# One stationary block for both parts of the sample tokens, and one ones-product per norm, in a two-layer hybrid decoder step

## What is computed

```python
def rmsnorm(x, g):
    y = x32 * lax.rsqrt(jnp.mean(x32 * x32, axis=-1, keepdims=True) + NORM_EPS)
    return (y * g).astype(x.dtype)

def token_mixer(h, ...):
    hq, hf, hi, hg, nq, kc, vc, ks, vs, kw, vw, ngate, mgate = jnp.split(h @ w_in, splits, axis=-1)
    o_hg = hgrn2_mixer(hq, hf, hi, hg, ...)      # gated linear attention, 4 heads; hi are its values
    o_nsa = ...                                  # attention over compressed, selected and window keys
    return merged @ w_out
x = x + token_mixer(rmsnorm(x, norm_mix[l]), ...)
x = x + conv_ffn(rmsnorm(x, norm_ffn[l]), ...)
```

## Time and profile before

| | us |
|---|---|
| median of 3 runs | 1172.31 |
| the runs | 1170.33 to 1174.61 |
| profiled execution, first to last instruction (span) | 1170.5 |
| TensorE busy | 1152.3 |
| VectorE busy | 706.3 |
| ScalarE busy | 544.3 |
| GpSimd busy | 173.2 |
| DMA, mean share of the 16 engines | 45% |

### The profile page before, as it was taken

One profiled execution on the slowest core, in us unless ns is written; L12 is line 12 of the kernel. 1 busy time (PEld: TensorE's weight loads), 2 busy tenths in 40 slices (PEclk: granted clock), 3 DMA queues, 4 the chain that ended last, 5 costly groups with the idle time before them and its releaser, 6 DMA issues.

```text
span 1170.5 us, 21146 instructions
## 1 busy us (share of the span) xinstructions
PE 1152.3 (98%) x8625; PEld 1039.7 (89%) x8625; DVE 706.3 (60%) x1303; ACT 544.3 (47%) x867; POOL 173.2 (15%) x300
## 2 busy tenths in 40 slices
PE   8999999999999999999999999999999999999997
PEld 6987776778999999999999787677899999999997
DVE  5686355557566777763568643544756677776442
ACT  4542265553355555533444234755534555554231
POOL 1154300011120001000114450000312111010000
PEclk7999999989999999999999999999999999999998
DMA  9554332347644444334456525213784445432401
GB/s 282 159 163 173 107 113 73 109 118 206 226 144 144 144 146 150 123 123 159 144 127 206 175 78 173 73 37 100 217 268 155 138 151 163 152 109 90 174 32 45
DMA packets 151498, 165.99 MB, mean 142 GB/s; under 512 B 31492, under 2 KB 114214, under 8 KB 151078
## 3 DMA queue, kind: packets, MB, share of 16 engines
q1 hardware_dynamic: 151402, 164.64, 45.0%
HBM read 156.22 MB, written 12.46 MB: 144 GB/s over the span
## 4 chain that ended last, share of the span: by engine, by line
PE 94%; DVE 2%; DMA 2%; ACT 1%; SPq 1%; issue 0%; DVEq 0%; ACTq 0%
PE mm L671 66%; PE ax L671 23%; PE ax L674 4%; DMA ring<-in_state_hgrn 1%; DMA ring<-in_state_conv 1%; ACT mixb L1328 1%; DVE ring_low L1684 0%; DVE mixb L1835 0%; DVE mixb L2100 0%; SPq L481 0%; DVE work_parts L2069 0%; PE mm L674 0%; DVE mixb L1852 0%; DVE mixb L2101 0%; DVE mixb L2254 0%
## 5 line engine op out<-in xcount | busy, mean ns | idle before, releaser
L671 PE MATMUL mm<-work_parts 128*128 128x320 f32 (+2 forms) x1120 | 357.4, 319 | 1.1 <-DVE h_low L1678 1.1
L1684 DVE TENSOR_TENSOR ring_low<-ring,work_parts 128x2048 fp32r<-128x2048 f32 (+2 forms) x116 | 256.0, 2207 | 125.3 <-ACT work_parts L1328 124.6
L671 PE MATMUL mm<-h_low,work_parts 128*128 128x320 f32 x1024 | 320.1, 313 | 0.0
L671 PE MATMUL mm<-work_parts,ring_low 128*128 128x320 f32 x1024 | 316.2, 309 | 0.0
L1328 ACT ACTIVATE work_parts<-ring 128x2048 fp32r<-128x2048 f32 (+2 forms) x116 | 211.9, 1827 | 159.7 <-PE mm L671 90.3
L671 PEld LDWEIGHTS mm<-work_parts 128*128 128x128 f32 (+1 forms) x1120 | 209.8, 187 | 9.4 <-issue 2.2
L671 PEld LDWEIGHTS mm<-h_low,work_parts 128*128 128x128 f32 x1024 | 193.7, 189 | 0.3
L671 PEld LDWEIGHTS mm<-work_parts,ring_low 128*128 128x128 f32 x1024 | 193.8, 189 | 0.0
L671 PE MATMUL ax<-act_parts,work_parts 128*128 128x320 f32 x544 | 127.3, 312 | 0.6 <-DVE ring L2091 0.6
L671 PE MATMUL mm<-act_parts,work_parts 128*128 128x320 f32 x480 | 117.4, 310 | 0.0
L671 PE MATMUL mm<-hT,ring 128*128 128x320 f32 x384 | 110.4, 439 | 0.0
(11 more groups left out here) (238 smaller groups left out, 1597.1 us busy)
## 6 DMA issues: line engine op xcount, KB each, us to landing
ring<-in_w_gate_up SPq DMA_DIRECT2D x44, 1024.0 KB, 6.6
ring<-in_w_in SPq DMA_DIRECT2D x10, 2048.0 KB, 8.5
ring<-in_w_in SPq DMA_DIRECT2D x18, 1024.0 KB, 5.5
ring<-in_w_down SPq DMA_DIRECT2D x8, 1536.0 KB, 6.7
ring<-in_w_out SPq DMA_DIRECT2D x4, 2048.0 KB, 13.9
ring<-in_w_down SPq DMA_DIRECT2D x4, 2048.0 KB, 8.0
ring<-in_w_in SPq DMA_DIRECT2D x32, 128.0 KB, 3.1
ring<-in_cache_cmp_kv SPq DMA_DIRECT2D x32, 128.0 KB
```

Source lines behind the costliest of these rows:

```text
L671: return nc.tensor.matmul(out, lhsT, rhs, start=start, stop=stop)
L1684: V.tensor_tensor(unit_of(u, ring_r), unit_of(u, ring), unit_high(u).bitcast(F32), ALU.subtract).then_inc(*st.up(w_low[l]))
```

## The change

`token_rows` takes the sample block another way. GpSimd copies the sample columns of `h_high` and `h_low` side by side into `row_parts` (64 and 64 columns per feature tile). They are one stationary block of 128 columns, and one product with the high weights and one with the low weights take the place of three. The bank's upper 64 partitions then hold what the low activations gave; ScalarE writes them, scaled, and VectorE adds the scaled lower 64 (`sample_rows`). So VectorE now empties `hi2` and `kvn2`. (The fourth product, low by low, is added to the sum by this.) `row_scales` makes the sample factors twice, one under the other. The rest concerns the norms: GpSimd adds all eight squares, one product with ones is left, and that of norm 1 moves from ahead of `hf1` into the middle of it.

```diff
-NADD = 6
-    ... [(f"{x}{i}", "A") for x in ("hi", "kvn", "kvc") for i in range(3)]
+    out += [(f"{x}{i}", "V" if i == 2 and x != "kvc" else "A") for x in ("hi", "kvn", "kvc") for i in range(3)]
...
 def norm1_sums():                                   # square_sums (norm 2) likewise
                 pe.wait_ge(squares_added, 2 * L + 1)
-                mm(bank[:, 0:T], ones, sq[:, NADD - 1, :], True, False)
-                for k in range(NADD, KD):
-                    pe.wait_ge(squares[L], k + 1)
-                    last = mm(bank[:, 0:T], ones, sq[:, k, :], False, k == KD - 1)
-                last.then_inc(ax_full[L], 1)
+                mm(bank[:, 0:T], ones, sq[:, KD - 1, :], True, True).then_inc(ax_full[L], 1)
...
 def token_rows(name, u0, half):
+                pe.wait_ge(row_parts_ready, L + 1)
                 pe.wait_ge(w_low[L], u + 1)
...
-                        last = split_products(bank[0:TM[i], :], h_high[:, k, rows], h_low[:, k, rows], high[:, kk, :],
-                                              low[:, kk, :], k == 0, k == KD - 1)
+                        if i < 2:
+                            last = split_products(bank[:, :], h_high[:, k, rows], h_low[:, k, rows], high[:, kk, :],
+                                                  low[:, kk, :], k == 0, k == KD - 1)
+                        else:
+                            mm(bank[:, :], sample_parts(k), high[:, kk, :], k == 0, False)
+                            last = mm(bank[:, :], sample_parts(k), low[:, kk, :], False, k == KD - 1)
...
 def row_scales():
-                for i in range(3):
-                    last = mm(bank[0:TM[i], i:i + 1], rs[:, P * i:P * i + TM[i]], ident[:, 0:1], True, True)
+                for i in range(2):
+                    mm(bank[:, i:i + 1], rs[:, P * i:P * i + P], ident[:, 0:1], True, True)
+                for y in range(2):
+                    last = mm(bank[SMP * y:SMP * y + SMP, 2:3], rs[:, SEQ:T], ident[:, 0:1], True, True)
...
 # TensorE, order of a layer
                 entry_tile("hf0", 0, 0, (entry_lo[L], 0))
-                norm1_sums()
                 for h in range(1, HH):
-                    entry_tile(f"hf{h}", h // 2, h % 2)
+                    entry_tile(f"hf{h}", h // 2, h % 2, None, norm1_sums if h == 1 else None)
...
 # ScalarE
+                def sample_rows_high(out, bank):
+                    A(out, bank[SMP:P, :], ACT.Copy, scale=rsc[SMP:P, 6:7]).then_inc(*st.up(high_rows[L]))
...
 # VectorE
+                def sample_rows(name, n, out):
+                    bank = take(MM[L], f"{name}2")
+                    ve.wait_ge(high_rows[L], n)
+                    V.scalar_tensor_tensor(out, bank[0:SMP, :], rsc[0:SMP, 6:7], out, ALU.mult, ALU.add).then_inc(
+                        *st.up(mm_dve[L]))
...
                     if 3 <= kk < 6:
                         split(HIU + kk - 2, l)
+                    if kk == 5:
+                        sample_rows("hi", 1, vH[0:SMP, 2, :])
                     if kk == 6:
...
+                        sample_rows("kvn", 2, stok[0:SMP, 2, :])
...
 # GpSimd
-                    for m in range(1, NADD):
+                    for m in range(1, KD):
...
                 link(G.memset(rH[:, :, :], 1.0))
+                po.wait_ge(entry_lo[L], KD)
+                for n, tiles in enumerate((slice(0, 6), slice(6, KD))):
+                    for x, src in enumerate((h_high, h_low)):
+                        last = G.tensor_copy(row_parts[n][:, :, x, :], src[:, tiles, SEQ:T])
+                last.then_inc(*st.up(row_parts_ready))
```

More of the change, by code:

```diff
@@ L116, in mm_plan @@
     out = [("par", "V")] + [(f"hf{h}", "V") for h in range(HH)] + [(f"hq{h}", "V") for h in range(HH)]
-    out += [(f"nq{m}", "V") for m in range(4)] + [(f"{x}{i}", "A") for x in ("hi", "kvn", "kvc") for i in range(3)]
+    out += [(f"nq{m}", "V") for m in range(4)]
+    out += [(f"{x}{i}", "V" if i == 2 and x != "kvc" else "A") for x in ("hi", "kvn", "kvc") for i in range(3)]
     out += [(f"hg{h}", "V") for h in range(HH)]
@@ L334, in hybrid_step, with sample_parts @@
         act_high, act_low = (part(act_r, NJ * T * n, NJ * T).rearrange("p (j t) -> p j t", j=NJ) for n in range(2))
+        row_parts = [nc.alloc_sbuf_tensor_at(f"row_parts{n}", [P, P * kn], F32R, offset=at)[:, :].rearrange(
+            "p (k x t) -> p k x t", k=kn, x=2) for n, (kn, at) in enumerate(((6, work_at + 4 * 8256), (2, mixb_at + 4 * 14080)))]
+        def sample_parts(k):
+            return row_parts[k // 6][:, k % 6].rearrange("p x t -> p (x t)")
         xin = part(mixb, 4096, 3 * D).rearrange("p (i c) -> p i c", i=3)
@@ L419, in hybrid_step @@
         s_ready, sn_ready, sqo_ready = lsem("state_ready"), lsem("new_state"), lsem("o_squares")
+        high_rows = lsem("sample_rows_of_high_parts")
         decayed, merged_ready, pre_ready = lsem("state_decayed"), lsem("merged_ready"), lsem("prefix_ready")
@@ L429, in hybrid_step @@
         oh_ready, sums_ready, rso_ready = sem("oh_parts_ready"), sem("o_square_sums"), sem("o_rs")
+        row_parts_ready = sem("sample_row_parts_ready")
         oh_raw, glast_ready = sem("oh_raw"), sem("glast_ready")
@@ L760, in split_products, with split_tile @@
                 return mm(out, low, x_high, False, stop)
-            def split_tile(R, name, u, h, x_high, x_low, tile_ready=None):
+            def split_tile(R, name, u, h, x_high, x_low, tile_ready=None, between=None):
                 bank = begin(R, name)
@@ L768, in split_tile @@
                         pe.wait_ge(tile_ready[0], tile_ready[1] + k + 1)
+                    if between is not None and k == kn // 2:
+                        between()
                     last = split_products(bank[:, 0:T], unit_high(u)[:, k, h, :], unit_of(u, ring_r)[:, k, h, :],
@@ L815, in row_scales, with entry_tile @@
                 pe.wait_ge(rs_ready[L], 1)
-                for i in range(3):
-                    last = mm(bank[0:TM[i], i:i + 1], rs[:, P * i:P * i + TM[i]], ident[:, 0:1], True, True)
+                for i in range(2):
+                    mm(bank[:, i:i + 1], rs[:, P * i:P * i + P], ident[:, 0:1], True, True)
+                for y in range(2):
+                    last = mm(bank[SMP * y:SMP * y + SMP, 2:3], rs[:, SEQ:T], ident[:, 0:1], True, True)
                 last.then_inc(ax_full[L], 1)
-            def entry_tile(name, u, h, tile_ready=None):
+            def entry_tile(name, u, h, tile_ready=None, between=None):
                 pe.wait_ge(w_low[L], u + 1)
-                split_tile(MM[L], name, u, h, h_high, h_low, tile_ready)
+                split_tile(MM[L], name, u, h, h_high, h_low, tile_ready, between)
             def queries(m):
@@ L1410, in layer @@
                     bank = take(MM[L], f"hi{i}")
-                    A(vH[0:TM[i], i, :], bank[0:TM[i], :], ACT.Copy, scale=rsc[0:TM[i], 4 + i:5 + i]).then_inc(
-                        *st.up(mm_act[L]))
+                    if i < 2:
+                        A(vH[:, i, :], bank[:, :], ACT.Copy, scale=rsc[:, 4 + i:5 + i]).then_inc(*st.up(mm_act[L]))
+                    else:
+                        sample_rows_high(vH[0:SMP, 2, :], bank)
                 split(KVU + 1, l)
@@ L1416, in layer @@
                     bank = take(MM[L], f"kvn{i}")
-                    A(stok[0:TM[i], i, :], bank[0:TM[i], :], ACT.Copy, scale=rsc[0:TM[i], 4 + i:5 + i]).then_inc(
-                        *st.up(mm_act[L]))
+                    if i < 2:
+                        A(stok[:, i, :], bank[:, :], ACT.Copy, scale=rsc[:, 4 + i:5 + i]).then_inc(*st.up(mm_act[L]))
+                    else:
+                        sample_rows_high(stok[0:SMP, 2, :], bank)
                 cached_rows(range(4, NSEQ))
@@ L1914, in layer @@
                         bank = take(AXR[L], "rst")
-                        V.tensor_copy(rsc[:, 4:6], bank[:, 0:2])
-                        V.tensor_copy(rsc[0:SMP, 6:7], bank[0:SMP, 2:3]).then_inc(*st.up(ax_dve[L]))
+                        V.tensor_copy(rsc[:, 4:7], bank[:, 0:3]).then_inc(*st.up(ax_dve[L]))
                     if h == 0:
@@ L2273, in squares_up_to_added @@
                 def squares_up_to_added(ready):
-                    for m in range(1, NADD):
+                    for m in range(1, KD):
                         po.wait_ge(ready, m + 1)
                         last = G.tensor_tensor(sq[:, m, :], sq[:, m - 1, :], sq[:, m, :], ALU.add)
-                        if m + 1 < NADD:
+                        if m + 1 < KD:
                             link(last)
```

## The result

| | before | changed |
|---|---|---|
| median of 20 runs, us | 1171.96 (1166.75 to 1175.96) | 1162.87 (1157.28 to 1170.04) |
| ratio | 1 | 0.9936, 95% interval 0.9921 to 0.9951 |
| profiled execution: span, mean granted clock | 1170.5, 0.985 | 1166.8, 0.979 |

The time lies in the stated range, 1.9 us above the forecast. By the ratio the gain is 7.5 us (5.7 to 9.3), by the medians 9.1, where 11.3 were forecast.

A forecast was written before the change was run, and what follows sets the result against it. TensorE's program, end to end, was taken as the time. Products 7.4 plus norms 4.3 minus row factors 0.4 gave 11.3 us off: 1172.3 - 11.3 = 1161.0 us, range 1157.5 to 1165.5.

The forecast's parts named there:

- The sum: TensorE's program gets shorter by 7.4 (products) + 4.3 (norms) - 0.4 (row factors) = 11.3 us.
- Products: Halves of `hi` and `kvn`: 32 products of 512 columns fall away at 0.231 us each, 7.4 us.
- The norms' pieces: Norms 1 and 2, both layers: two of three ones-products go, 1.07 us a norm, 4.3 us in all.
- row_scales: Row factors on TensorE: two more records cost 0.18 us, 0.4 us in two layers.
- Added work at nothing: New work on GpSimd and VectorE, and norm 1's move, are covered by spare time and add 0 us.
- the copies: Four GpSimd copies, at most 2.8 us, fit into its 25.92 us wait and add nothing.
- VectorE's instructions: Two new VectorE instructions a layer, for `hi` and `kvn`, taken at 0.78 us each, delay nothing TensorE needs.
- the move of norm 1: Norm 1's product stands 12 products later; the spare time ahead of `hq` shrinks from 1.5 to 0.5 us, no wait.
- norm 2's adds: Two more GpSimd adds at norm 2: sum ready 1.0 us before TensorE needs it; cost taken as 0.
- State wait: TensorE's wait for the states' DMA, 3.0 us in two waits, moves with TensorE; longer than 1.6 would be wrong.
- the other engines take some of it back: Rival, chance 0.16: chains behind three 0.6 us margins a layer and norm 2 run late; about 1164 us.
- The clock falls at another place: Rival: one clock fall costs 3.1 us; undone gives 1158 (chance 0.08), one more gives 1164 (0.08).

The follow-up runs named there:

- late: Changed kernel with VectorE's new instruction for `hi` ahead of the last low part of `kvn`'s weights instead of behind it; 1161.0 us, one execution.
- norm1_back: Changed kernel with norm 1's product ahead of `hf1` again; run twice, 1158.00 us (ratio 0.9915) and 1163.54 us (0.9923).
- norms_only: Kernel before with only the norms' part: eight squares added on GpSimd, one ones-product, norm 1's product inside `hf1`; 1167.12 us, ratio 0.9972.
- rows_only: Changed kernel with the norms of before, so only the sample tokens' two parts as one stationary block; 1162.33 us, ratio 0.9925.
- fill_before: Kernel before plus three products that nobody reads, ahead of TensorE's wait for the second half of the states; 1167.09 us, ratio 0.9965.

## Why the prediction came out as it did

- **The sum**: right for the products, too high for the rest. Products -7.4 counted, -7.4 measured with the rows part alone. The norms' pieces are each 1.07 us shorter in every chain, 4.3 in all, but only 3.4 show in the time at equal clock. `row_scales` was priced 0.4 and costs nothing. Whole change: 11.3 counted, 10.6 measured. With what the traces show, 7.4 + 4.3 - 0.6 for norm 1's adds - 0.5 for the states' wait gives the 10.6; the agreement to the tenth is luck, given the uncertainties.
- **Added work at nothing**: right for the copies, for VectorE's instructions (late shows their margin), for the move of norm 1 (norm1_back) and for norm 2's adds, whose sum stands at 350.54 us in the changed kernel, 1.0 ahead of TensorE, as counted. Wrong for norm 1's two adds. The prediction asked only whether GpSimd's sum comes in time, and only for norm 2; it left out that they now run at the same time as VectorE's first low part and `h_low`, slow these down, and so make TensorE wait some 0.6 us longer ahead of `hf0`.
- **State wait**: it was taken to move with TensorE unchanged. In the five profiles of the full change (with late) it is 3.2 to 4.1 us, 3.5 on average, against 3.0. The growth is all in the second layer: 1.65 to 2.79 us in the eight profiles that have the rows' part and no added products, against 1.48 before and 1.44 in norms_only. It costs about 0.5 us, a wait that the prediction had at nothing; two profiles without the rows' part are few, and why the DMA doesn't move along was not tried.
- **The rivals**: "the other engines take some of it back" (0.16) happened to the extent of some 0.6 us, but not at one of the margins that it names. "The clock falls at another place" did, to the worse side, which had 0.08. The result, 1162.9, lies between the forecast's 1161 within 1.5 and the 1164 of these two.
- **What was off is the size of the gain**, in the step that took 11.3 us off and left the clock and the waits as they were ("so the time is 1172.3 - 11.3"). The larger term missing there is the clock: over 39 executions the changed kernel spends 5.7 us more at the lower level, 2.3 us of time, and 10.6 - 2.3 = 8.3 us is the difference of the means, 1170.9 and 1162.6 (it has to be, the fit uses the same executions). In the first 20, on which the result stands, 38.4 us at the lower level against the 30 of the kernel before take 3.4 of the 10.8 back. (Its own 20 beside them have no clock on record; their mean time, 1171.4 us, is near the 1170.9 of the 45.) The smaller is the two waits, about 1.1 us, of which 0.4 is made up by `row_scales`.
- **Open**: why the whole change spends more time at the lower clock. Neither part alone does (29.5 and 29.0 us against 30.0), and the excess differs from occasion to occasion. In the profiles a fall begins between 148 and 150 us in every kernel that has the norms' part, and in neither before nor rows_only (fill_before, without that part, has one that begins at 152); but norms_only has it at no worse a mean clock, so it isn't the whole cause.

## What to carry to other kernels

In this kernel, which one engine bounds end to end, the products removed were time removed, one for one, as each neighbour's margin (its result's end to the bound engine's need) was larger than what was taken out ahead of it. Read those margins before, and put new work behind, not ahead of, what the bound engine waits for next. Work added on an engine with time to spare has a second price besides its own lateness: here two adds on GpSimd slowed the VectorE instructions that ran at the same time, and TensorE waited for those. So look also at what the neighbours do in that stretch. Where the clock has two levels, compare executions by span and mean clock together: two medians of six differed by 5.5 us for one program. A wait of TensorE could here be filled with products that nobody reads, at no cost that can be told.

## Not expected

- The spread of this kernel's times, 1157 to 1170 us, is nearly all the granted clock: 0.41 us per us at the lower level, 0.9 us left.
- With a wait of 1.5 us filled, no fall of 7 to 10 us came behind it in the profiles (0 of 8 places against 9 of 20).
- Two adds of 0.88 us each on GpSimd, which has time to spare, cost TensorE 0.6 us by way of VectorE.
